# Recurrence of the second block: keys and removal keys of a head loaded as one stationary of 128 columns

## What is computed

```
def step(state, inp):
    r_t, w_t, k_t, v_t, kh_t, a_t = inp
    removed = jnp.einsum('zhvk,zhk->zhv', state, kh_t)
    state = (state * w_t[:, :, None, :] - removed[..., None] * (kh_t * a_t)[:, :, None, :]
             + v_t[..., None] * k_t[:, :, None, :])
    return state, jnp.einsum('zhvk,zhk->zhv', state, r_t)
```

## Time and profile before

| | |
|---|---|
| median of 3 runs | 1980.43 us (1979.87 to 1981.43) |
| profiled execution | 1981.74 us |
| its span | 1979.8 us |
| TensorE matmul, busy | 1949.6 us, 98% of the span |
| VectorE, busy | 1125.0 us, 57% |
| ScalarE, busy | 469.2 us, 24% |
| recurrence in the span | about 1248 to 1470 us |

### The profile page before, as it was taken

One profiled execution on the slowest core, in us unless ns is written; L12 is line 12 of the kernel. 1 busy time (PEld: TensorE's weight loads), 2 busy tenths in 40 slices (PEclk: granted clock), 3 DMA queues, 4 the chain that ended last, 5 costly groups with the idle time before them and its releaser, 6 DMA issues.

```text
span 1979.8 us, 35835 instructions
## 1 busy us (share of the span) xinstructions
PE 1949.6 (98%) x14899; PEld 1358.7 (69%) x14899; DVE 1125.0 (57%) x1894; ACT 469.2 (24%) x906; POOL 249.7 (13%) x239
## 2 busy tenths in 40 slices
PE   8999999999999999999999999999999999999997
PEld 6778979964778878995445565999985444444443
DVE  2697385654569657655668848545457333233324
ACT  3164110000426311000231145432333111110111
POOL 4684000000568100000000012000000000000000
PEclk9999999999999999999999999999998999999999
DMA  8333545544533355535821334200012999999995
GB/s 261 128 128 107 213 141 168 161 178 147 191 128 128 107 213 170 169 129 197 317 78 60 117 128 167 92 4 3 3 48 112 378 428 428 428 428 428 428 428 222
DMA packets 138891, 385.56 MB, mean 195 GB/s; under 512 B 16986, under 2 KB 64450, under 8 KB 127622
## 3 DMA queue, kind: packets, MB, share of 16 engines
q1 hardware_dynamic: 138757, 383.61, 51.6%
HBM read 382.55 MB, written 1.05 MB: 194 GB/s over the span
## 4 chain that ended last, share of the span: by engine, by line
PE 91%; DVE 7%; issue 1%; ACT 1%; DMA 0%; DVEq 0%; POOL 0%; ACTq 0%
PE psum L713 13%; PE psum L416 11%; PE psum L1754 10%; PE psum L3466 10%; PE psum L2629 8%; PE psum L3491 5%; PE psum L755 5%; PE psum L3396 3%; PE psum L438 3%; PE psum L609 3%; PE psum L3523 2%; PE psum L674 2%; PE psum L771 2%; PE psum L689 1%; PE psum L3042 1%; PE psum L2686 1%
## 5 line engine op out<-in xcount | busy, mean ns | idle before, releaser
L416 PE MATMUL psum<-arena,ring 128*128 128x256 f32 x1472 | 326.1, 380 | 0.0
L416 PEld LDWEIGHTS psum<-arena,ring 128*128 128x128 f32 x1472 | 276.0, 189 | 46.1 <-issue 7.2
L2629 PE MATMUL psum<-arena 64*64 64x64 f32 (+1 forms) x4320 | 179.7, 238 | 2.7 <-issue 1.5
L2629 PEld LDWEIGHTS psum<-arena 64*64 64x64 f32 x4320 | 171.4, 134 | 4.7 <-issue 2.7
L713 PE MATMUL psum<-arena,ring 128*128 128x128 f32 x1280 | 149.5, 275 | 0.0
L713 PEld LDWEIGHTS psum<-arena,ring 128*128 128x128 f32 x1280 | 146.1, 192 | 0.0
L1754 PE MATMUL psum<-arena,ring 128*128 128x512 f32 (+2 forms) x432 | 142.0, 490 | 0.0
L822 ACT ACTIVATE arena<-psum 128x512 f32<-128x512 f32 (+2 forms) x80 | 42.0, 544 | 348.5 <-PE psum L416 119.4
L1754 PEld LDWEIGHTS psum<-arena,ring 128*128 128x128 f32 (+1 forms) x432 | 81.1, 188 | 60.7 <-issue 55.4
L713 PE MATMUL psum<-arena 128*128 128x128 f32 x960 | 113.7, 274 | 0.0
L713 PEld LDWEIGHTS psum<-arena 128*128 128x128 f32 x960 | 110.4, 192 | 0.0
(11 more groups left out here) (517 smaller groups left out, 3104.6 us busy)
## 6 DMA issues: line engine op xcount, KB each, us to landing
ring<-in_w_in_dram SPq DMA_DIRECT2D x29, 2048.0 KB, 8.0
ring<-in_ffn_w_dram SPq DMA_DIRECT2D x46, 1024.0 KB, 7.8
arena<-in_ex_gate_dram SPq DMA_DIRECT2D x15, 2048.0 KB, 16.6
arena<-in_ex_up_dram SPq DMA_DIRECT2D x15, 2048.0 KB, 21.0
arena<-in_ex_down_dram SPq DMA_DIRECT2D x15, 2048.0 KB, 21.6
ring<-in_ex_gate_dram SPq DMA_DIRECT2D x14, 2048.0 KB, 13.9
ring<-in_ex_up_dram SPq DMA_DIRECT2D x14, 2048.0 KB, 18.3
ring<-in_ex_down_dram SPq DMA_DIRECT2D x14, 2048.0 KB, 20.4
```

What stands on the lines that cost most here:

```text
L416: ins = pe.matmul(bank[:, j, :], w[:, kc, c * P:(c + 1) * P], moving[:, kc, :], start=kc == 0, stop=kc == k - 1)
L2629: ins = pe.matmul(bank[r, u, :], a[r, u], b[r, u], start=i == 0, stop=i == len(terms) - 1)
```

## The change

The groups `mr` and `nr` become two groups `("kb", r)`, one for each of the two heads of a pair. Their stationary is the keys and the removal keys of one head side by side, 64 rows by 128 columns; the product lands on all 128 partitions, keys' product in the lower 64 (`K_ROWS`), removal keys' in the upper 64 (`B_ROWS`). `kb` is laid out with the pair u outermost for this. The tiles that the products go to stay as they were, so each eviction of `mr` and `nr` becomes two of 64 partitions, and half of them move the data to the other half of the partitions. In the list of groups `kb` of r = 0 stands at the place of `mr` and `kb` of r = 1 at that of `nr`. The core of the diff:

```
-                keys += [("mr", c, z), ("m", c, z), ("nr", c, z)]
+                keys += [("kb", 0, c, z), ("m", c, z), ("kb", 1, c, z)]
...
-        each(("mr", c, z), 2, (t.b, kr))
+        for r in range(2):
+            pe.wait_ge(K.empty(("kb", r, c, z)), K.empty_count(("kb", r, c, z)))
+        for u in range(HP):
+            for r, rows in enumerate(HEAD_ROWS):
+                ins = pe.matmul(by_two(K.bank(("kb", r, c, z)))[:, u], t.kb[rows, u].rearrange("p i t -> p (i t)"), kr[rows, u], start=True, stop=True)
+                if u == HP - 1:
+                    ins.then_inc(K.full(("kb", r, c, z)), 1)
...
-        each(("nr", c, z), 2, (t.k, kr))
...
                 act.wait_ge(K.sem["strict"], strict - 1)
-                copy(("mr", c, z), t.own(c, BT), by_two(K.bank(("mr", c, z)))[:, :, 1, :])
+                for r, rows in enumerate(HEAD_ROWS):
+                    act.wait_ge(K.full(("kb", r, c, z)), K.full_count(("kb", r, c, z)))
+                    act.activation(t.own(c, BT)[rows], by_two(K.bank(("kb", r, c, z)))[B_ROWS, :, 1, :], ACT.Copy)
...
                 act.wait_ge(K.sem["pairs"], turn_of(c, z))
-                copy(("nr", c, z), t.own(c, KT), by_two(K.bank(("nr", c, z)))[:, :, 1, :])
+                for r, rows in enumerate(HEAD_ROWS):
+                    copy(("kb", r, c, z), t.own(c, KT)[rows], by_two(K.bank(("kb", r, c, z)))[K_ROWS, :, 1, :])
...
-        key = ("mr", c, z)
-        dve.wait_ge(K.full(key), K.full_count(key))
-        ins = tt_op(t.strict_out(c, lat), by_two(K.bank(key))[:, :, 0:n, :], spread(K.masks[:, z, 0:n, :]), ALU.mult)
-        ins.then_inc(K.empty(key) if lat else K.sem["strict"], 1)
+        for r, rows in enumerate(HEAD_ROWS):
+            key = ("kb", r, c, z)
+            dve.wait_ge(K.full(key), K.full_count(key))
+            tt_op(t.strict_out(c, lat)[rows], by_two(K.bank(key))[B_ROWS, :, 0:n, :], spread(K.masks[B_ROWS, z, 0:n, :]), ALU.mult).then_inc(
+                K.sem["strict"], 1)
...
-        key = ("nr", c, z)
-        dve.wait_ge(K.full(key), K.full_count(key))
-        ins = tt_op(t.pairs_out(c, lat), by_two(K.bank(key))[:, :, 0:n, :], spread(K.masks[:, z, 0:n, :]), ALU.mult)
-        ins.then_inc(K.empty(key) if lat else K.sem["pairs"], 1)
+        for r, rows in enumerate(HEAD_ROWS):
+            key = ("kb", r, c, z)
+            ins = tt_op(t.pairs_out(c, lat)[rows], by_two(K.bank(key))[K_ROWS, :, 0:n, :], spread(K.masks[K_ROWS, z, 0:n, :]), ALU.mult)
+            if lat:
+                ins.then_inc(K.empty(key), 1)
+                dve.wait_ge(K.empty(key), K.drained_count(key))
+        if lat:
+            dve.sem_inc(K.sem["pairs"], 1)
+        else:
+            ins.then_inc(K.sem["pairs"], 1)
...
-        self.kb = self.kb_and_one[:, 0:2 * HP, :].rearrange("p (i u) t -> p i u t", i=2)
+        self.kb = self.kb_and_one[:, 0:2 * HP, :].rearrange("p (u i) t -> p u i t", i=2)
```

More of the change, by code:

```diff
@@ L1673 @@
 )
-CHUNK_EVENTS = dict(wkv_tiles=2, one_ready=1, decay=CHUNKS * ZS, hats=CHUNKS * ZS, inv_start=CHUNKS * ZS, strict=(CHUNKS + LAT) * ZS,
-                    pairs=LAT * ZS)
+CHUNK_EVENTS = dict(wkv_tiles=2, one_ready=1, decay=CHUNKS * ZS, hats=CHUNKS * ZS, inv_start=CHUNKS * ZS, strict=3 * CHUNKS * ZS,
+                    pairs=CHUNKS * ZS)
 TAIL_EVENTS = dict(
@@ L2594, in strict_of @@
 def strict_of(c, z):
-    return 2 * turn_of(c, z) if c < LAT else turn_of(c, z) + LAT * ZS
+    return 3 * turn_of(c, z)
 def grown_by(n, c, z):
@@ L2667, in level @@
         if n == 1:
-            if c >= LAT:
-                drained(("mr", c, z))
             pe.wait_ge(K.sem["strict"], strict_of(c, z))
@@ L2697, in values @@
     def values(c, z):
[L2698 to L2701, removed]
         t = K.wkv[z]
+        pe.wait_ge(K.sem["pairs"], turn_of(c, z))
         each(("nv", c, z), 1, (t.nk[:, :, 0, :], values_at(c, z)))
@@ L2713, in moved @@
         t = K.wkv[z]
-        drained(("wu", c, z), ("t1" if c >= LAT else "mr", c, z))
+        drained(("wu", c, z), *([("t1", c, z)] if c >= LAT else [("kb", r, c, z) for r in range(2)]))
         if c == CHUNKS - 1:
@@ L2728, in outputs @@
         else:
-            drained(("wu", c, z), ("mr", c, z))
-        if c < LAT:
-            drained(("nr", c, z))
+            drained(("wu", c, z))
+        drained(*[("kb", r, c, z) for r in range(2)])
         if c >= LAT:
@@ L2822, in wkv_vector @@
     tt_op, stt = dve.tensor_tensor, dve.scalar_tensor_tensor
-    spread = lambda a: a.unsqueeze(1).broadcast_to([P, HP, *a.shape[1:]])
+    spread = lambda a: a.unsqueeze(1).broadcast_to([a.shape[0], HP, *a.shape[1:]])
     def hats(c, z):
@@ L2834, in hats @@
             tt_op(kr[:, :, 1, :], K.r_T[:, :, at - T:at - T + CH], upto, ALU.mult)
-        tt_op(t.kb, K.k_and_a[:, :, :, at:at + CH], t.p_inv.unsqueeze(1).broadcast_to([P, 2, HP, CH]), ALU.mult).then_inc(K.sem["hats"], 1)
+        tt_op(t.kb.rearrange("p u i t -> p i u t"), K.k_and_a[:, :, :, at:at + CH], t.p_inv.unsqueeze(1).broadcast_to([P, 2, HP, CH]), ALU.mult).then_inc(K.sem["hats"], 1)
     def inner(c, z):
@@ L2847, in inner @@
             K.sem["strict"], 1)
-        if lat:
-            dve.wait_ge(K.empty(key), K.drained_count(key))
-        else:
-            dve.wait_ge(K.sem["strict"], strict_of(c, z) - 1)
+        dve.wait_ge(K.sem["strict"], strict_of(c, z) - 1)
         tt_op(t.inv, t.powers(0)[:, :, 0, :], spread(K.one), ALU.add).then_inc(K.sem["inv_start"], 1)
@@ L3860, in __init__ @@
         self.zero, self.inv, self.zero_and_inv = self.x[:, :, 0, :], self.x[:, :, 5, :], self.x[:, :, 0:6:5, :]
-        self.k, self.b = self.kb[:, 0], self.kb[:, 1]
+        self.k, self.b = self.kb[:, :, 0, :], self.kb[:, :, 1, :]
     def powers(self, n):
@@ L3889, in b_and_one @@
     def b_and_one(self, u):
-        return self.kb_and_one[:, HP + u:2 * HP + 1:HP - u, :]
+        return self.kb_and_one[:, 2 * u + 1:2 * HP + 1:2 * HP - 1 - 2 * u, :]
     def power_and_inv(self, n):
@@ L3902 @@
 RB, BT, KT, KRT, NV = range(5)
+K_ROWS, B_ROWS = HEAD_ROWS
 def flat(a):
```

## The result

| | before | after |
|---|---|---|
| median | 1980.38 us (6 runs, 1979.61 to 1982.39) | 1989.45 us (6 runs, 1986.01 to 1992.4) |
| span of the profiled execution | 1979.8 us | 1987.7 us |

The ratio is 1.0039 with a 95% interval of 1.0029 to 1.0050: slower by 7.7 us, interval 5.7 to 9.9 (the two medians are 9.1 us apart). The forecast was 1985.6, range 1982.0 to 1989.0, slower with 0.73. The sign is right; the first median is 0.45 us above the range, the second inside it.

The account below looks back on a forecast made before the run. The prediction took TensorE to bound the recurrence. Gains of 8.25 us against waits of 13.5 us gave net +5.2 us, on 1980.43 a forecast of 1985.6 us, range 1982.0 to 1989.0.

Parts of the forecast that it names:

- What bounds it: In the recurrence TensorE is the limit; its gains and waits at a chunk's start count one to one.
- TensorE's gain: mr and nr, 1.74 us per chunk and direction, become kb at 1.24; 1.01 gained a chunk, 8.25 us in all.
- both rivals about them: At kb on TensorE: shape change free, 1982.3 us, chance 0.07; row halves not running together, 2000 us, chance 0.03.
- The waits: At chunk starts TensorE waits for kb's banks until VectorE or ScalarE has taken the keys out: 13.5 us in all.
- the walk: VectorE's eviction list timed from each chunk's start, giving waits and net +5.2 us; chance 0.82, own range +2.5 to +8.
- The walk's two waits in chunk 0: In context chunk 0: 0.42 us at nv, 0.86 behind ScalarE's first-level copy; 1.28 against a gain of 1.18, net +0.10.
- No bank waits: Rival: at t1 and st TensorE finds the bank free and the whole 8.25 us gain comes, 1972.2 us; chance 0.04.
- The clock: Rival: six long waits in the recurrence each cost 1.5 us at 1.2 GHz, +9, 1995 us; chance 0.04.
- The sum: Over the recurrence: gains 8.25, waits 13.5, net +5.2 us, carried to the whole time as 1985.6 us.

Follow-up runs that it names:

- the versions with other banks: Changed kernel with groups behind kb given other banks, in latent, context or all chunks: 1984.56, 1984.55 and 1977.00 us; ratios to before 1.0010, 1.0010 and 0.9978.
- the banks of waiting groups moved: Changed kernel with early-wanted groups on the banks of m and gr, late ones on kb's, in all chunks: 1977.00 us, ratio to before 0.9978.
- The delay of 5.2 us without any wait: Kernel before with TensorE repeating the m group of direction 0 in chunks 1 to 6: 1988.85 us, ratio to before 1.0040.
- the second series: The changed kernel, unaltered, timed and profiled again: 1987.92 us against 1981.91 for the kernel before, ratio 1.0031.
- 1.7 us more: Kernel before with TensorE repeating one m group in context chunks 1 and 2 only: 1984.89 us, ratio to before 1.0011.
- latent banks moved: Changed kernel with the groups behind the first eight on other banks in latent chunks only: 1984.56 us, ratio to before 1.0010.

## Why the prediction was right, and where it was off

**What bounds it.** Right. TensorE's issue is the limit, and every gain and every wait at the start of a chunk went into the recurrence one to one, by the table of chunks and by the versions with other banks.

**TensorE's gain.** `kb` stands for 1.09 us from its first start to `m` and `m` for 1.02 where it was 0.87, together 1.24 for `kb` with its change forth and back. Measured without the waits the gain is 1.01 to 1.02 in chunks 1 to 6 (25.21 to 24.20, 31.03 to 30.01), where 1.01 was the term. The two row halves run together (0.11 for each step), the change is charged 0.35: both rivals about them fall.

**The waits.** A direction was to take 2.98 us on TensorE and takes 1410.21 - 1407.23 = 2.98. VectorE's list from the second direction's removal keys to `t1` was to take 7.73 - 4.29 = 3.44 us and takes 1414.78 - 1411.34 = 3.44. The halves of 512 elements are 0.72 apart (1411.34, 1412.06, 1412.79), half-partition evictions are no shorter. Here the sentence of the Trainium skill that the walk drew on (VectorE: DVE Perf Modes, Two Vector instructions with no wait between them) agrees with the trace at every one of these places, also at 256 elements: two halves of different partitions are 0.42 to 0.46 apart, two of the same 0.33. The groups by shape show the durations:

```profile
L2645 PE MATMUL psum<-arena 64*128 64x128 f32 x256 | 18.6, 285 | 0.4 <-ACT arena L2082 0.4
...
L2859 DVE TENSOR_TENSOR arena<-psum,arena 64x512 f32<-64x512 f32 x16 | 10.9, 680 | 0.9
...
L2859 DVE TENSOR_TENSOR arena<-psum,arena 64x256 f32<-64x256 f32 x16 | 6.6, 414 | 0.2
```

The four waits at `t1` sum to 6.5, the walk's 3 x 1.77 and 1.93 to 7.2; but idle time in this view is shorter than the delay of a start, since a matmul's end is modelled. By starts, the delay in chunk 6 is 1.81.

**The beginning.** By the rows of the table the walk was good to 0.06 us, chunk 0 among them; the 0.42 by which the whole recurrence misses it (5.64 against 5.22) lie at its two ends. What the walk left out is the bank of `kb`, r = 1, in the very first chunk. A group of work ahead of the recurrence still holds it, so TensorE waits 0.36 us before its first `kb` (timeline of TensorE; the other two waits are those walked for chunk 0):

```profile
1249.31 1.16 PE L2645 MATMUL psum<-arena 64*128 64x128 f32 x16 [0.36 <-ACT arena L2082]
...
1255.71 1.15 PE L2629 MATMUL psum<-arena 64*64 64x64 f32 x32 [0.25 <-ACT arena L2783]
1257.52 8.26 PE L2629 MATMUL psum<-arena 64*64 64x64 f32 x192 [0.66 <-ACT arena L2783]
```

That wait is the larger part of the 0.42. The walk's two waits in chunk 0 come to 1.28 us and by starts to 1.3, but their parts were off: some 0.3 at `nv` instead of 0.42, and 1.0 at the second level instead of 0.86.

**No bank waits.** This rival falls as a forecast for this kernel. With the banks of waiting groups moved most of its 8.25 us come: the rows of chunks 1 to 6 save 1.01 to 1.02 us each, that of chunk 0 still loses 0.33, the two ends together save 0.7. The recurrence is 6.5 us shorter and the time 1977.0 in its series, 5.0 under before.

**The clock.** I gave this rival 0.04 with the argument that a stretch with 1.6 us idle in 5 had kept 1.00. That argument was too weak. In one of two profiles of the changed kernel the clock did fall behind two of the six long waits, for 1.56 us each; the price I had named was 1.5. So this rival was right in part, and that the first profile, by which the walk is judged here, kept the full clock is luck: in the second the recurrence is 9.1 us longer than before and not 5.6.

**The sum.** +5.2 forecast for the recurrence, +5.64 measured. The step that carried this to the whole time, "nothing after the recurrence is running early", is true of the work but leaves out that the clock behind the recurrence isn't a constant: the rest of the span was 1756.3 to 1768.5 us in twelve profiles of kernels whose code there is the same, and it goes with the granted clock, 0.98 to 0.85. From the profile with 0.98 to that with 0.85 are 27 us at half clock and 12.2 us of time. The delay of 5.2 us without any wait made the median 6.9 higher, the changed kernel's 5.6 us made it 9.1 and 6.0 in two series. So whatever stands above the recurrence's own 5.6 us comes without `kb` too. It is small against the noise: the interval of the second series (3.8 to 8.5) contains 5.6, that of the first begins at 5.7. That a later start is its cause isn't shown, and the profiles speak against it as the only one (same end of the recurrence, other stretches; ends 16 us apart, same rest). The single profiles and the medians of a kernel do not always agree either (1.7 us more: a shorter span in the profile, a longer median). What decides where the clock falls stays open.

## What to carry to other kernels

When groups of products are merged, look at who gives back their bank and how late in its list: here some 8 us of gain on TensorE were turned into a loss because the bank of the merged group was the next one wanted and its last reader stood at the end of VectorE's list. Walk the evicting engine's list with start-to-start distances, change of half partitions and all; it was good to 0.06 us in each of the seven rows. Walk the first chunk too: whoever worked before it may still hold a bank. Then try another assignment of banks before giving up the change: reordering up to 8 keys of the list per chunk turned +0.39% into -0.22% [-0.32, -0.13].

## What the runs showed of the hardware that was not expected

- The granted clock in the 100 us behind the recurrence: between 3.4 and 31 us at 1.2 GHz per execution in kernels that do the same there, with up to 12 us of span, and the runs of one kernel differ in their mean clock (1977.75 us at 0.997 and 1989.34 at 0.99, latent banks moved).
- A wait of TensorE of 2 us was followed by 3.4 us at 1.2 GHz in one execution and by none in another of the same kernel.
- ScalarE too is slower to follow in copies that change the half of the partitions. Its 64-partition copies of 256 elements start 0.39 to 0.40 us apart (the two below take 0.77), whole copies of 256 elements in the kernel before 0.33 to 0.34 (the two below take 0.72). I had counted on 0.33; in the walk only one of them was on the path. No run has two ScalarE copies of the same half behind each other, so that the change of half is the reason isn't shown. First the changed kernel, then the one before:

```profile
1251.39 0.77 ACT L2792 ACTIVATE arena<-psum 64x256 f32<-64x256 f32 x2 [2.23 <-DVE arena L2846]
```

```profile
1300.28 0.72 ACT L2784 ACTIVATE arena<-psum 128x256 f32<-128x256 f32 x2 [1.28 <-DVE arena L2859]
```
